# A hybrid decoder trunk: memory columns split without GpSimd, and memory chunks split while TensorE works on the chunk ahead

## What is computed

```python
proj = rmsnorm(h, mix_norm[l]) @ w_in[l]
# three mixers read proj: a state-space group (scan), 6 heads of latent
# attention, 6 heads of sparse attention (compressed, selected, window)
h = h + concat(rmsnorm(y_ssm), rmsnorm(y_mla), rmsnorm(y_nsa)) @ w_out[l]
# cross-attention: 4 heads into 256 memory tokens
kv = (rmsnorm(mem, mem_norm[l]) @ wkv).reshape(bsz, m, 2, 4, 256)
h = h + softmax(q @ k.T / 16) @ v @ wo
h = h + swiglu(...)            # dense on layer 0, 2 of 8 experts on layer 1
```

## Time and profile before

| | us |
|---|---|
| median of 3 runs (1858.77 to 1860.43) | 1859.87 |
| the profiled execution's own time | 1859.66 |
| its span in the trace | 1857.8 |
| PE busy, share of the span | 1704.5, 92% |
| DVE busy | 1337.5, 72% |
| ACT busy | 1083.8, 58% |
| POOL busy | 229.9, 12% |

### The profile page before, as it was taken

One profiled execution on the slowest core, in us unless ns is written; L12 is line 12 of the kernel. 1 busy time (PEld: TensorE's weight loads), 2 busy tenths in 40 slices (PEclk: granted clock), 3 DMA queues, 4 the chain that ended last, 5 costly groups with the idle time before them and its releaser, 6 DMA issues.

```text
span 1857.8 us, 24338 instructions
## 1 busy us (share of the span) xinstructions
PE 1704.5 (92%) x8492; PEld 1420.9 (76%) x8492; DVE 1337.5 (72%) x1499; ACT 1083.8 (58%) x1196; POOL 229.9 (12%) x258
## 2 busy tenths in 40 slices
PE   6699899799987998996999999999999999999995
PEld 5667787688877677875788888888888888888784
DVE  5556554544555565554889898998999988989895
ACT  4344533444343435433777777777777777777773
POOL 1944000000029340003000000000000000000200
PEclk8889999899998898996999999999999999999998
DMA  9301332755533013422999999999999999999992
GB/s 361 137 16 54 114 136 95 316 191 192 191 135 115 23 46 113 142 108 100 380 371 381 380 377 380 376 373 385 374 380 367 377 386 381 372 375 361 408 364 110
DMA packets 68696, 475.94 MB, mean 256 GB/s; under 512 B 7543, under 2 KB 9079, under 8 KB 13976
## 3 DMA queue, kind: packets, MB, share of 16 engines
q1 hardware_dynamic: 63816, 453.01, 64.0%
q0 software_dynamic: 4816, 22.08, 3.0%
HBM read 461.82 MB, written 13.24 MB: 256 GB/s over the span
## 4 chain that ended last, share of the span: by engine, by line
PE 79%; DVE 6%; POOL 6%; ACT 4%; issue 2%; DMA 2%; DVEq 0%; POOLq 0%; ACTq 0%; SPq 0%
PE bank L430 22%; PE bank L432 22%; PE bank L431 22%; POOL big L2125 3%; ACT upper L469 1%; PE bank L612 1%; DMA skewed_bias<-big 1%; PE bank L1458 1%; PE bank L1367 1%; DVE xel L944 1%; POOL memraw L2170 1%; POOL small L2125 1%; POOL attn L2125 1%; DVE lower L475 1%; PE bank L1437 1%
## 5 line engine op out<-in xcount | busy, mean ns | idle before, releaser
L475 DVE TENSOR_TENSOR lower<-ring,upper 128x2048 fp32r<-128x2048 f32 x369 | 845.5, 2292 | 144.9 <-ACT upper L469 131.2
L469 ACT ACTIVATE upper<-ring 128x2048 fp32r<-128x2048 f32 x369 | 706.0, 1914 | 115.6 <-PE bank L432 108.4
L430 PE MATMUL bank<-upper,xeu 128*128 128x512 f32 x896 | 361.0, 403 | 6.8 <-DVE xel L944 3.4
L432 PE MATMUL bank<-upper,xel 128*128 128x512 f32 x896 | 351.4, 392 | 0.0
L431 PE MATMUL bank<-lower,xeu 128*128 128x512 f32 x896 | 350.6, 391 | 0.0
L430 PE MATMUL bank<-upper,htu 128*128 128x512 f32 x536 | 209.6, 391 | 4.9 <-DVE htl L958 3.4
L432 PE MATMUL bank<-upper,htl 128*128 128x512 f32 x536 | 208.7, 389 | 0.0
L431 PE MATMUL bank<-lower,htu 128*128 128x512 f32 x536 | 208.6, 389 | 0.0
L430 PEld LDWEIGHTS bank<-upper,xeu 128*128 128x128 f32 x896 | 168.9, 189 | 39.4 <-DVE lower L475 4.4
L432 PEld LDWEIGHTS bank<-upper,xel 128*128 128x128 f32 x896 | 168.9, 188 | 36.2
L431 PEld LDWEIGHTS bank<-lower,xeu 128*128 128x128 f32 x896 | 169.4, 189 | 32.0
(11 more groups left out here) (376 smaller groups left out, 2599.1 us busy)
## 6 DMA issues: line engine op xcount, KB each, us to landing
ring<-in_weights SPq DMA_DIRECT2D x423, 1024.0 KB, 5.7
routed_rows<-g POOLq DMA_DIRECT2D x1, 4096.0 KB, 30.1
lp<-in_lparams POOLq DMA_DIRECT2D x1, 3634.5 KB, 11.9
lp<-in_lparams SPq DMA_DIRECT2D x1, 3584.0 KB, 29.4
memraw<-routed_rows POOLq DMA_DIRECT2D x7, 512.0 KB, 6.1
expert_rows<-xk POOLq DMA_DIRECT2D x7, 512.0 KB, 8.8
skewed_bias<-big SPq DMA_DIRECT2D x1, 1152.0 KB, 19.3
row<-in_mem SPq DMA_DIRECT2D x1, 1024.0 KB, 5.1
```

The source lines that it names most:

```text
L430: pe.matmul(to, x_up, w_up, start=start, stop=False, skip_group_check=True)
L432: return pe.matmul(to, x_lo, w_up, start=False, stop=stop, skip_group_check=True)
L469: act.activation(upper[:, q % 3, :], ring[:, q % RING, :], ACT.Copy).then_inc(done, 1)
L475: dve.tensor_tensor(lower[:, q % RING, :], ring[:, q % RING, :], f32(upper[:, q % 3, :]), ALU.subtract).then_inc(done, 1)
```

## The change

POOL's memory work is gone. ACT makes the upper parts straight from `memraw`, scaling on the way, in eight copies of 256 columns; in layer 1 it waits for `mem_back` itself. DVE makes the lower parts in eight `scalar_tensor_tensor` (memory block times gain minus upper part), each after ACT's copy, between the copy of `vs` and `hid`. PE's wait before the head loop counts eight of them.

In the head loop, at i = 2, 6, 10 and 14 ACT now takes exponentials i+3 first, then makes the upper part of the chunk after the one that PE works on (8, 9, 10, 11), and then drains the `mk` product and `pT`i. DVE makes the matching lower part in the same step, after masked scores i+3. Chunk 12 is split after the loop on both engines.

```diff
--- before.py
+++ after.py
@@ -342,7 +342,6 @@
         wt_split = lsem("wt_split")
         tr_upper = lsem("tr_upper")
         row_ready = lsem("row_ready")
-        mem_scaled = lsem("mem_scaled")
         mem_upper = lsem("mem_upper")
         mem_split = lsem("mem_split")
         rope_ready = lsem("rope_ready")
@@ -1383,7 +1382,7 @@
 
                 for i in range(LEAD):
                     scores(i)
-                pe.wait_ge(mem_split[l], 4)
+                pe.wait_ge(mem_split[l], KD)
                 for i in range(HEADS):
                     if i + LEAD < HEADS:
                         scores(i + LEAD)
@@ -1570,10 +1569,10 @@
                 A(z[:, 0, 192:320], z[:, 0, 192:320], ACT.Copy, scale=rstd[:, 4:5])
                 A(z[:, 1, 192:320], z[:, 1, 192:320], ACT.Copy, scale=rstd[:, 5:6]).then_inc(z_ready[l], 1)
                 wait_tile(act, l, "vs")
-                for i in range(4):
-                    a = slice(i * 512, (i + 1) * 512)
-                    act.wait_ge(mem_scaled[l], 2 * i + 2)
-                    A(colrf[:, a], memrawf[:, a], ACT.Copy).then_inc(mem_upper[l], 1)
+                if l:
+                    act.wait_ge(mem_back, 16)
+                for k in range(KD):
+                    A(colr[:, k, :], memraw[:, k, :], ACT.Copy, scale=cols[:, C_MEM + k:C_MEM + k + 1]).then_inc(mem_upper[l], 1)
                 wait_tile(act, l, "cqT")
                 A(ql[:, 0, :], bank("cqT")[:, 0:256], ACT.Copy, scale=cols[:, C_QN:C_QN + 1])
                 drained(A(ql[0:64, 1, :], bank("cqT")[0:64, 256:512], ACT.Copy, scale=cols[0:64, C_QN + 1:C_QN + 2]))
@@ -1619,22 +1618,17 @@
                 for i in range(HEADS):
                     if i in MEMK:
                         m = MEMK[i]
+                        exponentials(i + LEAD)
+                        layer_chunk_upper(act, l, MEM_FIRST + m + 1)
                         wait_tile(act, l, f"mk{m}")
                         drained(A(xk[:, 2 * m:2 * m + 2, :], bank(f"mk{m}")[:, :], ACT.Copy))
-                    if i in MEMK and MEMK[i] >= 1 and MEMK[i] + 1 < XH:
-                        layer_chunk_upper(act, l, MEM_FIRST + MEMK[i] + 1)
                     wait_tile(act, l, f"pT{i}")
                     if i >= 2:
                         act.wait_ge(pe_note[l], i - 1)
                     drained(A(pt[:, i % 2, 0:384], bank(f"pT{i}")[:, 0:384], ACT.Copy))
-                    if i + LEAD < HEADS:
+                    if i + LEAD < HEADS and i not in MEMK:
                         exponentials(i + LEAD)
-                    if i + LEAD == NH:
-                        layer_chunk_upper(act, l, MEM_FIRST + 1)
-                    if i + LEAD == HEADS - 1:
-                        layer_chunk_upper(act, l, MEM_VALUES)
-                    if i == HEADS - 2:
-                        layer_chunk_upper(act, l, MEM_VALUES + 1)
+                layer_chunk_upper(act, l, MEM_VALUES + 1)
 
                 def memory_values(m):
                     for t in range(TT):
@@ -1908,6 +1902,11 @@
                                                      ALU.mult, ALU.add)
                     ins.then_inc(scan_ready[l], 1)
 
+                dve.wait_ge(mem_back if l else mem_kept, 16)
+                for k in range(KD):
+                    dve.wait_ge(mem_upper[l], k + 1)
+                    dve.scalar_tensor_tensor(memr[:, k, :], memraw[:, k, :], cols[:, C_MEM + k:C_MEM + k + 1],
+                                             f32(colr[:, k, :]), ALU.mult, ALU.subtract).then_inc(mem_split[l], 1)
                 wait_tile(dve, l, "hid")
                 b = bank("hid")
                 for v in range(2):
@@ -1995,19 +1994,19 @@
                             dve.wait_ge(o_read[l], TT * n + t + 1)
                             link(tt(to, to, x, ALU.add))
 
-                LOWERS = {4: MEM_FIRST + 1, 8: MEM_FIRST + 2, 12: MEM_FIRST + 3, 15: MEM_VALUES, 17: MEM_VALUES + 1}
                 for i in range(LEAD):
                     masked_scores(i)
                 layer_chunk_lower(dve, l, MEM_FIRST)
                 for i in range(HEADS):
                     if i + LEAD < HEADS:
                         masked_scores(i + LEAD)
-                    if i in LOWERS:
-                        layer_chunk_lower(dve, l, LOWERS[i])
+                    if i in MEMK:
+                        layer_chunk_lower(dve, l, MEM_FIRST + MEMK[i] + 1)
                     if i in STATES:
                         states(STATES[i])
                     if i in (NH, 2 * NH):
                         group_outputs(i // NH - 1)
+                layer_chunk_lower(dve, l, MEM_VALUES + 1)
                 group_outputs(2)
 
                 dve.wait_ge(g_free[l], 8)
@@ -2161,18 +2160,6 @@
                 power(2, 4, rstd_ready[l])
                 link(double(64))
                 double(128).then_inc(ftab_ready[l], 1)
-
-                if l:
-                    pool.wait_ge(mem_back, 16)
-                else:
-                    pool.wait_ge(mem_kept, 16)
-                for k in range(KD):
-                    pool.tensor_scalar(memraw[:, k, :], memraw[:, k, :], cols[:, C_MEM + k:C_MEM + k + 1], None,
-                                       ALU.mult).then_inc(mem_scaled[l], 1)
-                for i in range(4):
-                    a = slice(i * 512, (i + 1) * 512)
-                    pool.wait_ge(mem_upper[l], i + 1)
-                    tt(memrf[:, a], memrawf[:, a], f32(colrf[:, a]), ALU.subtract).then_inc(mem_split[l], 1)
 
                 for j in range(8):
                     pool.wait_ge(scan_ready[l], j + 1)
```

## The result

| | median us (range) | profiled execution: span, granted clock |
|---|---|---|
| before | 1859.94 (1858.77 to 1860.43) | 1857.8, 0.956 |
| after | 1818.64 (1816.14 to 1820.99) | 1817.0, 0.968 |

The changed kernel is faster: ratio 0.978 (95% interval 0.9765 to 0.9796), 41.3 us off the median and 40.8 off the profiled span.

The account below looks back on a forecast made before the run. PE bounds the kernel, waiting for ql behind ACT's wait for POOL, and losing head-loop time to waits and lower clock. 13.7 + 20.2 = 33.9 us off 1859.66 gives 1825.8; range 1817 to 1841, forecast's own 1820 to 1832.

Parts of the forecast that it names:

- The STTs take turns with the doublings: Ahead of the head loop: DVE's STTs and POOL's table doublings exclude each other, one instruction each in turn.
- Rival A: No exclusion on POOL's doublings, or DVE slips in unhindered: memory-column work gives 20 us, time 1819.5; chance 0.15.
- Each doubling put off by one whole STT (0.36 us): Rotation table on POOL: six STTs delay it from 83.4 to 85.6 in layer 0; states(0) starts at 87.0.
- Part 1: Memory columns without POOL, ahead of the head loop: vm1 ends 6.9 and 6.8 us sooner, 13.7 us in all.
- vm1 to the first score "the same chain as before": Behind vm1: gelu, kcv and compressed scores follow as before, no gain; a lower clock could cost 3 us.
- Head loop: Earlier memory-chunk splits: loop near 67 us, clock above 0.93, no waits behind mk2 and mk3, about 1 us at outputs(12).
- (b)+(c): Head loop, per layer: shorter wait of outputs(12) for the group output, 2.2 us; full clock up to mk3, 1.8 us.
- (d)+(e): Per layer: from mk3's end to the first value product 4.2 us gained; first six value products closer together, 1.0.
- Rival C: PE waits anew between kn1, vm0 and vm1, keeps the lower clock to the loop: 1841.7; chance 0.12.
- Rival D: Head loop: split chain exposed, mk drains over 1 us late with PE idle, 5.5 us per chunk: 1890; chance 0.04.
- Rival E: Waits for POOL and splits go, but PE waits as long for another input there: 1859.7; chance 0.02.
- "The stages behind shift whole": Stages behind the attention keep their length, starting from full ring slots, so the whole gain reaches the end: 1825.8.

Follow-up runs that it names:

- psum: Changed kernel with the second tensor of DVE's eight STTs read from a PSUM bank, upper part not subtracted: 1820.86 us, ratio 0.979 to before.
- after_again: The changed kernel measured once more, without any edit: 1820.22 us, ratio 0.978 to before.
- undo_b: Changed kernel with only chunk 3's lower part put back ahead of the group output in the head loop: 1830.03 us, ratio 0.9839 to before.
- undo_d: Changed kernel with only the split of the first value chunk put back behind mk3's drain: 1828.98 us, ratio 0.9837 to before.
- warm_after: Changed kernel with 14 products of constants on PE between qn0 and qr0 of layer 0: 1820.44 us, ratio 0.9778 to before.
- pool: Changed kernel with the memory columns' lower parts subtracted on POOL in idle time, ACT scaling in place: 1816.38 us, ratio 0.9767 to before.
- warm_before: Kernel before with 30 (layer 1: 20) products of constants on PE between bu0 and qn0: 1856.25 us, ratio 0.9982.

## Why the prediction was right, step by step

- **PE's wait at L1302.** Gone from qn0, moved to qr0, 6.88 us, under the 9 foretold. Right, with its cause (the table).
- **The STTs take turns with the doublings.** Right: 14.01 us for eight in layer 0, 10.28 in layer 1, and 3.22 with a PSUM input (psum). Rival A's mechanism is refuted, though its time, 1819.5, is nearer than mine.
- **Each doubling put off by one whole STT (0.36 us).** This size was wrong. Six doublings lost 0.9 us together, 0.15 each. The table ended at 84.3, not 85.6, and states(0) started at 85.46, not 87.0; in layer 1 17.7 us sooner than before, which against vs, 20.4 us sooner there, is 2.7 later where 3.5 was foretold. I had read the turns off short instructions on both engines, where a wait for the other is as long as the other's instruction; against a POOL instruction of 2 us DVE pays nearly the whole of it, and POOL only a part of the STT. That isn't because POOL never pays. In the trace of before a doubling whose neighbours take 0.24 us or less starts with a lower part of DVE and takes as long as that:

```profile
43.75 2.29 DVE L454 TENSOR_TENSOR lower<-ring,upper 128x2048 fp32r<-128x2048 f32 x1
```

```profile
43.76 2.36 POOL L2125 TENSOR_TENSOR big<-big,attn 128x16 f32<-128x16 f32 x1
```

- **Rotations.** 4.26 us (88.75 to 93.01) for the 4.75 taken; the slowing that I allowed for was half as large. vm1 ended at 96.2 for 97.4 foretold. Part 1 to vm1: 16.3 us, not 13.7, and this is 2.6 of the 7.4 us missing.
- **vm1 to the first score "the same chain as before".** This step failed: for both layers it took 4.1 us less in this profile. Its bound for an unknown clock there was one-sided, a loss of 3 us. The trace of before had the answer within reach: a stretch of 14.17 us with 12.43 of PE work at a clock of 0.77 (the fence of before above, whose columns I did not use for the forecast) could also rise. It is the largest piece of what was missing, about 4 of 7.4. Layer 0's half of it came in all five kernels with this front, so it belongs to the change, though through what was not found; layer 1's half came in two of six, and after_again did not have it.
- **Head loop.** 67.07 us for the 67 foretold, 65.89 in layer 1; clock 0.97, above 0.93; no wait behind mk2 or mk3; outputs(12) waits 0.97 for 0.95 foretold. Both loops gave 20.1 and the values 2.3, 22.4 for the 20.2 of the sum. Terms (b)+(c) measure 4.9 and 3.7 (undo_b), (d)+(e) 3.9 and 5.1 (undo_d), with 1.7 us between the shortest and the longest of equal loops.
- **Late parts.** The last chunk's split and the group output cost nothing, as foretold. Rival C's new wait did come in layer 1 (2.22 us, ahead of L1310 at 580.37), and PE did not keep a low clock to the loop from it: the stretch behind stood at 0.90, the loop took 65.89. Rival D's sign is absent: the drains of mk2 and mk3 end within some 0.7 us of the chunk's last product (the row at 173.29). Rival E's would be a wait of PE on another input at the same places in the loop, and there is only the 0.97 us one.
- **"The stages behind shift whole".** Not quite: from the end of layer 1's value products to the end it is 1.7 us longer (1141.7 for 1140.0), mostly at a lower clock up to the expert stage. A granted clock of 0.81 stands before in the last 80 us ahead of that stage, 0.77 after. The change alone doesn't make it: after_again, the same kernel, has 1140.4 us and 0.81 there.

The miss of 7.4 us adds up: 2.6 to vm1, 4.1 behind it, 2.2 in loop and values, less 2 given back, 6.9, and the rest is between the profiled execution and the median.

Two of these pieces do not come with the change each time: the 1.9 us gained behind vm1 in layer 1 and the 1.7 lost behind the loops. They nearly cancel, and that is luck.

**Still open.** What decides whether the clock falls right behind the gap. It is not how early vm1 ends: in layer 0 psum and warm_after had it low and pool high, with vm1 sooner than in the change in all three. It is not full clock ahead of vm1 alone: warm_before had 0.68 in layer 0 and 0.89 in layer 1. The idle gap ahead of kcv was 2.46 us in every kernel that doesn't fill it.

## What to carry to other kernels

- Where PE waits for an engine that itself stands in a queue behind a third, move the third's work off the queue: the gain is the distance to the next hinge, which can be read off the trace before. Here ql had come at 92.5 and the table stood at 83.4 (84.3 in the end), and vm1 came 8 us sooner.
